# An attention pipeline's output stage: emitted in one piece, or one part per pipeline step

## The chip, the cores and the metric

The kernel runs on the 8 cores of one Trainium2 chip. Each core works on one of the 8 batch elements and exchanges nothing with the others. The metric is device time in microseconds of the slowest core for one execution.

## The reference

A backbone of four layers works on 4096 latent tokens and 256 context tokens per batch element, with 1024 channels. Layers 0 and 2 mix by a depthwise convolution beside a Fourier transform. Layers 1 and 3, which the change touches, do this:

```python
cb, cc, cx, cg, q, k, v, ag = _odd_proj(_pre(x, o_norm[i], sh, sc), o_w_in[i])
att = _window_attention(_apply_rope(q, cos, sin), _apply_rope(k, cos, sin), v, k_c, v_c, o_sink[i])
x = x + gt * _odd_out(cb, cc, cx, cg, att, ag, o_c_conv_w[i], o_w_out[i])

def _odd_out(cb, cc, cx, cg, att, ag, c_conv_w, w_out):
    y_c = cb * _dwconv(cc * cx, c_conv_w) * jax.nn.silu(cg)
    y_d = att * jax.nn.silu(ag)
    return jnp.concatenate([y_c, y_d], axis=-1) @ w_out
```

Attention has 8 query heads of 64 channels over 2 key heads. A query block of 128 tokens sees three key blocks of 128 around it, the 256 context keys, and a sink logit. In layer 1 the context tokens are updated too; in layer 3 they are not, and a final RMSNorm follows.

## The kernel before

An odd layer has two stages with a barrier between them. The first projects the inputs, block by block (8 blocks of 512 latent tokens, then one of 256 context tokens), and keeps keys and values in the on-chip memory. The second, in which everything here happens, is a software pipeline over units. A unit is one query block of 128 tokens and one head, so a full block of 512 tokens has 32 units; layer 1 has 272 units (the last 16 are the context's) and layer 3 has 256.

The loop at the end of `odd_layer` runs in steps. In step s it emits, in this order:

- `stA1(s)`: TensorE multiplies the mask, the keys and the context keys into two PSUM banks (the first matmul reads `mask_s` and stands at the start of a step in the trace); VectorE takes the row maximum (`TENSOR_REDUCE`, L1095); ScalarE takes the exponential (L153), from 642 columns.
- `stB(s-2)`: TensorE transposes the probabilities of unit s-2 in five pieces into bank 4 + (s % 2) (L143); they are copied out of that bank by ScalarE (`COPY`, L166), and for every third unit by VectorE (`COPY`, L168).
- `stC(s-4)`: TensorE multiplies the transposed probabilities with the values, five matmuls of 64 columns.
- whatever stands in `deferred` for that step.

Every engine works off its own instructions in order; a wait holds all that is queued behind it on that engine. The scheduler class adds the waits from the buffers that an operation reads and writes. A PSUM bank is one such buffer, so a matmul that opens a bank waits for the last reader of it. The semaphore of an engine counts its instructions in order.

After the eighth head of a query block, `fin2` is deferred by two steps: four transposes into bank 4 + (number of the query block % 2) and a VectorE multiplication into `mix`. For the last query block of a block, `fin2` also calls `stO3`, the output stage. It uses banks 4 and 5:

```python
for c in range(4):
    pc = bank(4 + c % 2)
...
out_stage(l, j, Wout, mx_, last, fin_bufs, banks=(4, 5))
```

These are four convolution pieces (3 matmuls of 512 columns and one VectorE multiplication each), eight output chunks (8 matmuls of 512 columns, then one `SCALAR_TENSOR_TENSOR` on VectorE, L162, that adds into `X`), then in layer 1 the store to `xres`, and in layer 3 the final norm: a square of 4096 columns on ScalarE, 32 matmuls of 2 columns, a square root on ScalarE, and for each of four token tiles eight transposes of 128 columns in single precision, two VectorE operations and a store. At last `load_block` fetches the inputs of the block after next over the GpSimd queue.

Of the kernel before, what the change touches and what calls it, by code (L numbers as in the profile page):

```python
# [10 lines left out]
AF = mybir.ActivationFunctionType  # L11
ALU = mybir.AluOpType
# [3 lines left out]
D = 1024  # L16
KC = 8
# [198 lines left out]
def build(L, LC, layers, dbg=False):  # L216
# [15 lines left out]
    s = Sched(nc)  # L232
# [8 lines left out]
    finbc_d = din("finbc", [128, D])  # L241
# [30 lines left out]
    out_d = nc.dram_tensor("out", [L, D], F32, kind="ExternalOutput").ap()  # L272
# [4 lines left out]
    xres = dscr("xres", [128, KC, T], F32)  # L277
# [10 lines left out]
    identf = sb("identf_s", [128, 128], F32)  # L288
    onesb = sb("onesb", [128, 128], BF16)
    ones512 = sb("ones512", [128, 128], BF16)  # L290
    epsc = sb("epsc", [128, 1], F32)
# [7 lines left out]
    modc = {l: sb("modc%d" % l, [128, 24, 2], F32) for l in layers}  # L299
# [15 lines left out]
    def bank(i):  # L315
        return PS[:, i * 512:(i + 1) * 512], bkb[i]

    ld = lambda out, in_, R, W: s.dma("sp", out, in_, R, W)
    st = lambda out, in_, R, W: s.dma("pool", out, in_, R, W)
# [162 lines left out]
                     e="act" if h == 0 else "dve")  # L482
        ld(xres.ap[:, :, t0:t0 + nt], xb.ap[:, :, :nt], [xb.b()], [xres.b(j)])

    def out_stage(l, j, Wout, mix, last, fin_bufs, banks=(4, 5, 6, 7), xb=None):
        stx, t0, nt = blocks[j]
        if xb is None:
            xb = X[j % 2]
        for m in range(KC):
            pb = bank(banks[m % len(banks)])  # L490
            p, b = pb
            for c in range(KC):
                s.mm(p[:, :nt], Wout.ap[:, c, m * 128:(m + 1) * 128], mix.ap[:, c, :nt], c == 0, c == KC - 1,
                     [Wout.b(), mix.b()], [b])
            s.stt(xb.ap[:, m, :nt], p[:, :nt], modc[l].ap[:, 16 + m, stx:stx + 1], xb.ap[:, m, :nt],
                  ALU.mult, ALU.add, [b, modc[l].b(), xb.b()], [xb.b()])
        if not last:
            st(xres.ap[:, :, t0:t0 + nt], xb.ap[:, :, :nt], [xb.b()], [xres.b(j)])
        elif stx == 0:
            finbc, sq, fst, TO = fin_bufs  # L500
            if not finbc.bufs:
                ld(finbc.ap, finbc_d, [], [finbc.b()])
            nti = nt // 128
            s.act(sq.ap[:, :, :nt], xb.ap[:, :, :nt], AF.Square, [xb.b()], [sq.b()])
            pss, pssb = bank(banks[-1])
            for i in range(nti):
                for c in range(KC):
                    s.mm(pss[:, 2 * i:2 * i + 2], sq.ap[:, c, i * 128:(i + 1) * 128], onesb.ap[:, 0:2],
                         c == 0, c == KC - 1, [sq.b(), onesb.b()], [pssb])
            s.act(fst.ap[:, 0:2 * nti], pss[:, 0:2 * nti], AF.Sqrt, [pssb, epsc.b()], [fst.b()],  # L510
                  bias=epsc.ap, scale=1.0 / D)
            s.op("dve", lambda e: e.reciprocal(fst.ap[:, 8:8 + 2 * nti], fst.ap[:, 0:2 * nti]), [fst.b()], [fst.b()])
            for i in range(nti):
                to = TO[i % 2]
                for h in range(2):
                    pt, ptb = bank(banks[-2 + h])
                    for c in range(4):
                        cc = h * 4 + c
                        s.tr(pt[:, c * 128:(c + 1) * 128], xb.ap[:, cc, i * 128:(i + 1) * 128], identf.ap,
                             [xb.b(), identf.b()], [ptb])  # L520
                    s.stt(to.ap[:, h * 512:(h + 1) * 512], pt, fst.ap[:, 8 + 2 * i:9 + 2 * i],
                          finbc.ap[:, h * 512:(h + 1) * 512], ALU.mult, ALU.mult,
                          [ptb, fst.b(), finbc.b()], [to.b()])
                st(out_d[t0 + i * 128:t0 + (i + 1) * 128, :], to.ap, [to.b()], [])

    def even_layer(l, last, nxt, first=False, win_pre=None):
        w = LW[l]
# [324 lines left out]
    def odd_layer(l, last, ctx_needed, nxt):  # L852
# [9 lines left out]
        sq = A.alloc([128, KC, 512], BF16)  # L862
# [33 lines left out]
        for j, (stx, t0, nt) in enumerate(blocks):  # L896
# [3 lines left out]
            h = hT[j % 2]  # L900
# [57 lines left out]
            for i in range(nt // 128):  # L958
                pt, ptb = bank(6 + i % 2)
# [11 lines left out]
        Wout = A.alloc([128, KC, D], BF16)  # L971
        diag = A.alloc([128, 4, 3, 128], BF16)
# [6 lines left out]
        mix = [A.alloc([128, 8, 512], BF16) for _ in range(2)]  # L979
# [3 lines left out]
        fin_bufs = None  # L983
        if last:
            fin_bufs = (A.alloc([128, D], F32), A.alloc([128, KC, 512], BF16), A.alloc([128, 16], F32),
                        [A.alloc([128, D], F32) for _ in range(2)])
# [17 lines left out]
        ablocks = [j for j, (stx, t0, nt) in enumerate(blocks) if stx == 0 or ctx_needed]  # L1004
# [9 lines left out]
        def load_block(j):  # L1014
            stx, t0, nt = blocks[j]
            sstart = 0 if stx == 0 else L
            send = L if stx == 0 else T
            xb = X[j % 2]
            st(xb.ap[:, :, :nt], xres.ap[:, :, t0:t0 + nt], [xres.b(j)], [xb.b()])
            gi = gDi[j % 2]  # L1020
            st(gi.ap[:, :, :nt], sB.ap[:, :, t0:t0 + nt], [sB.b(j)], [gi.b()])
            cbi = cbgi[j % 2]
            st(cbi.ap[:, :, :nt], sA.ap[:, :, t0:t0 + nt], [sA.b(j)], [cbi.b()])
            cxi = ccxi[j % 2]
            lo = max(t0 - 1, sstart)
            hi = min(t0 + nt + 1, send)
            nbr = [sC.b(jj) for jj in (j - 1, j, j + 1) if 0 <= jj < NB and blocks[jj][0] == stx]
            if lo == t0:
                s.op("dve", lambda e: e.memset(cxi.ap[:, :, 0:1], 0.0), [], [cxi.b()])
            if hi == t0 + nt:  # L1030
                s.op("dve", lambda e: e.memset(cxi.ap[:, :, nt + 1:nt + 2], 0.0), [], [cxi.b()])
            st(cxi.ap[:, :, lo - (t0 - 1):hi - (t0 - 1)], sC.ap[:, :, lo:hi], nbr, [cxi.b()])
# [31 lines left out]
        deferred = {}  # L1064
# [48 lines left out]
        def stC(u):  # L1113
            g = geom(u)
            j, qi, hh = g["j"], g["qi"], g["hh"]
            par, nk, hk = g["par"], g["nk"], g["hk"]
            o_ps, o_b = bank(6 + g["qbi"] % 2)
            vR = [Vf2.b(kb_) for kb_ in g["kbufs"]]
            nkt = nk // 128
            for t in range(nkt):  # L1120
                s.mm(o_ps[:, hh * 64:(hh + 1) * 64], pT_sb[u % 3].ap[:, t * 128:(t + 1) * 128],
                     Vf2.ap[:, g["ktiles"][t], hk * 64:(hk + 1) * 64], t == 0, t == nkt - 1,
                     [pT_sb[u % 3].b(0)] + vR, [o_b])
            if hh == 7:
                qbi = g["qbi"]
                sq_ = SQ[qbi % 2]
                asb = att_sb[qbi % 2]
                s.tt(asb.ap.rearrange("p (h d) -> p h d", h=8), o_ps.rearrange("p (h d) -> p h d", h=8),
                     sq_.ap[:, 5, :].unsqueeze(2).broadcast_to([128, 8, 64]), ALU.mult, [o_b, sq_.b(9)], [asb.b()])
                lastq = (qi == g["nt"] // 128 - 1)  # L1130

                def fin2(j=j, qi=qi, qbi=qbi, lastq=lastq):
                    asb_ = att_sb[qbi % 2]
                    mx_ = mix[j % 2]
                    gi = gDi[j % 2]
                    p7, p7b = bank(4 + qbi % 2)
                    p7v = p7.bitcast(BF16)
                    for c in range(4):
                        s.tr(p7v[:, c * 128:(c + 1) * 128], asb_.ap[:, c * 128:(c + 1) * 128], identb.ap,
                             [asb_.b(), identb.b()], [p7b])  # L1140
                    s.tt(mx_.ap[:, 4:8, qi * 128:(qi + 1) * 128], p7v[:, 0:512].rearrange("p (c q) -> p c q", c=4),
                         gi.ap[:, :, qi * 128:(qi + 1) * 128], ALU.mult, [p7b, gi.b()], [mx_.b()])
                    if lastq:
                        stO3(j)
                deferred.setdefault(u + 4 + 2, []).append(fin2)

        def stO3(j):
            stx, t0, nt = blocks[j]
            mx_ = mix[j % 2]
            cbi = cbgi[j % 2]  # L1150
            cxi = ccxi[j % 2]
            for c in range(4):
                pc = bank(4 + c % 2)
                for k in range(3):
                    s.mm(pc[0][:, :nt], diag.ap[:, c, k, :], cxi.ap[:, c, k:k + nt], k == 0, k == 2,
                         [diag.b(), cxi.b()], [pc[1]])
                s.tt(mx_.ap[:, c, :nt], pc[0][:, :nt], cbi.ap[:, c, :nt], ALU.mult, [pc[1], cbi.b()], [mx_.b()])
            out_stage(l, j, Wout, mx_, last, fin_bufs, banks=(4, 5))
            nx2 = ablocks.index(j) + 2
            if nx2 < len(ablocks):  # L1160
                load_block(ablocks[nx2])

        step = 0
        while step < NU + 4 or any(k >= step for k in deferred):
# [21 lines left out]
    for li, l in enumerate(layers):  # L1186
        last = (li == len(layers) - 1)
# [127 lines left out]
```

How the kernel before makes its waits and increments, by code:

```python
    def _wait(self, e, tok):  # L76
        k, sem, val, src = tok
        if src == "pe" and e == "pe":
            return
        if self.seen[e].get(k, 0) >= val:
            return
        self.eng[e].wait_ge(sem, val)
        self.seen[e][k] = val
# [19 lines left out]
    def op(self, e, fn, R=(), W=()):  # L103
        self._deps(e, R, W)
        inst = fn(self.eng[e])
        self.cnt[e] += 1
        inst.then_inc(self.sem[e], 1)
        self._commit((self.semk[e], self.sem[e], self.cnt[e], e), R, W)
# [1 line left out]
    def dma(self, q, out, in_, R=(), W=(), **kw):  # L110
        self._deps(q, R, W)
        i = self.rpos[q]
        self.rpos[q] = (i + 1) % self.NRING
        sem = self.ring[q][i]
        k = self.ringk[q][i]
        prev = self.rval[q][i]
        if prev:
            self._wait(q, (k, sem, prev, "dma"))
        inst = self.eng[q].dma_start(out=out, in_=in_, **kw)
        inst.then_inc(sem, 16)
        self.rval[q][i] = prev + 16
        self._commit((k, sem, prev + 16, "dma"), R, W)
```

## Time and profile before

| quantity | value |
| --- | --- |
| runs | 4970.52 and 5032.25 us, median 5001.38 us |
| profiled execution | 4973.7 us, span of its slowest core 4972.4 us |
| spans of the 8 cores | 4937.0 to 4972.4 us |
| TensorE busy | 3913.2 us (79%) |
| VectorE busy | 1979.7 us (40%) |
| ScalarE busy | 1661.6 us (33%) |
| mean granted TensorE clock, per core | 0.905 to 0.912 |

The profile is that of core 1. The attention pipeline of layer 1 lies between 1911 and 2530 us of its span, that of layer 3 between 4270 us and the end. A granted clock of 1.00 is the upper level of TensorE (2.4 GHz), 0.50 the lower (1.2 GHz).

### The profile page before, as it was taken

Reading aid. Unit: us, or ns where it says so; the run is one execution under the profiler, and the core shown is the slowest. Engines: PE = TensorE matmul, PEld = TensorE weight load, DVE = VectorE, ACT = ScalarE, POOL = GpSimd, SP = SyncE. Lnnn points to the kernel's source line nnn. Section 1 sums busy time; section 2 is a strip of 40 time slices with the busy share of each in tenths; the row PEclk is TensorE's granted clock in tenths of the full one; section 3 lists DMA queues with packets and bytes.
Section 4 is the critical chain, followed back from the end, with each engine's and each line's share of the span. In section 5 each row is a group of like instructions: output and inputs, shape, how many; then the busy total and the mean of one; then the engine's idle time right before and its main releaser. Section 6 shows DMA issues by size and latency. Waiting matters only on the chain.

```text
span 4972.4 us, 75994 instructions; the slowest of 8 cores (4937.0 to 4972.4 us)
## 1 busy us (share of the span) xinstructions
PE 3913.2 (79%) x26536; PEld 2224.8 (45%) x26536; DVE 1979.7 (40%) x3068; ACT 1661.6 (33%) x2642; POOL 465.0 (9%) x511
## 2 busy tenths in 40 slices
PE   2989599789569996777769959969874999577776
PEld 1444344665324444544434434456542444344454
DVE  1333344122235444656533333311222444455564
ACT  1545233000023334655535523310002333455463
POOL 1000000000101221000010000000001112100000
PEclk9999799899879998999879979979987999899888
DMA  8333212854552224332433221166436321321210
GB/s 154 123 127 106 51 44 49 253 182 170 152 130 89 89 68 109 120 112 78 112 109 104 77 56 43 49 205 221 161 140 138 106 89 64 96 101 54 94 61 37
DMA packets 223621, 537.60 MB, mean 108 GB/s; under 512 B 51024, under 2 KB 69840, under 8 KB 215056
## 3 DMA queue, kind: packets, MB, share of 16 engines
q0 software_dynamic: 103568, 323.02, 22.4%
q1 hardware_dynamic: 119680, 209.72, 13.1%
q8 instruction: 221, 3.62, 0.3%
q14 instruction: 152, 1.25, 0.1%
HBM read 424.94 MB, written 167.25 MB: 119 GB/s over the span
## 4 chain that ended last, share of the span: by engine, by line
PE 68%; DVE 8%; DMA 8%; issue 6%; ACT 5%; POOL 3%; another core or an unknown queue 1%; DVEq 0%; SPq 0%; POOLq 0%; ACTq 0%
PE ps L140 63%; PE ps L143 5%; ACT arena L153 4%; POOL arena L156 3%; DVE arena L156 3%; DMA arena<-sD 2%; DVE arena L159 1%; DMA X<-xres 1%; DVE arena L887 1%; DMA arena<-wmod 1%; DVE arena L162 1%; ACT arena L166 1%; DMA arena<-x 1%; DMA arena<-pqd 1%
## 5 line engine op out<-in xcount | busy, mean ns | idle before, releaser
L140 PE MATMUL ps<-arena 128*128 128x512 bf16 (+4 forms) x19564 | 3406.7, 328 | 372.6 <-DVE arena L156 111.6
L140 PEld LDWEIGHTS ps<-arena 128*128 128x128 bf16 x19564 | 1793.7, 100 | 1814.1 <-issue 556.1
L153 ACT ACTIVATE arena<-ps,biasW 128x512 f32<-128x512 f32 (+3 forms) x614 | 410.4, 671 | 725.3 <-PE ps L140 682.3
L153 ACT ACTIVATE arena<-ps,arena 128x642 bf16<-128x642 f32 (+2 forms) x528 | 414.4, 785 | 343.5 <-PE ps L140 186.9
L1095 DVE TENSOR_REDUCE arena<-ps 128x1 f32<-128x642 f32 (+2 forms) x528 | 424.5, 805 | 227.9 <-PE ps L143 111.4
L166 ACT COPY arena<-ps 128x640 bf16<-128x640 bf16 (+3 forms) x369 | 252.4, 684 | 766.0 <-PE ps L140 706.4
L156 DVE TENSOR_TENSOR arena<-ps,arena 128x512 bf16<-128x512 f32 (+4 forms) x328 | 215.9, 666 | 538.1 <-PE ps L140 231.0
L143 PE MATMUL ps<-identb_s,arena 128*128 128x128 bf16 x2892 | 282.4, 228 | 158.6 <-ACT arena L166 71.7
L162 DVE SCALAR_TENSOR_TENSOR X<-ps,modc,X 128x512 f32<-128x512 f32 (+1 forms) x280 | 203.8, 728 | 330.0 <-PE ps L140 327.7
L153 ACT ACT_TABLE_LOAD x156 | 200.1, 1283 | 354.7 <-PE ps L140 135.3
L162 DVE SCALAR_TENSOR_TENSOR arena<-ps,biasW,arena 128x512 bf16<-128x512 f32 (+1 forms) x208 | 149.1, 717 | 340.8 <-PE ps L140 275.3
L143 PEld LDWEIGHTS ps<-identb_s,arena 128*128 128x128 bf16 x2892 | 184.0, 101 | 219.7 <-issue 182.4
L140 PE MATMUL ps<-mask_s,identb_s 128*128 128x384 bf16 (+1 forms) x512 | 174.2, 340 | 128.0 <-ACT arena L153 111.5
L153 ACT ACTIVATE arena<-X 128x4096 bf16<-128x4096 f32 (+1 forms) x44 | 152.1, 3458 | 348.5 <-DMA X<-xres 173.6
L153 ACT ACTIVATE arena<-ps,v_s 128x512 f32<-128x512 f32 (+3 forms) x144 | 87.9, 662 | 444.0 <-PE ps L140 444.0
L162 DVE SCALAR_TENSOR_TENSOR arena<-X,G,ps 128x512 bf16<-128x512 f32 (+1 forms) x288 | 205.4, 713 | 19.4 <-DVE arena L162 1.4
L168 DVE CAST arena<-ps 128x512 bf16<-128x512 f32 (+2 forms) x74 | 46.8, 660 | 375.5 <-ACT arena L166 189.0
L156 DVE TENSOR_TENSOR arena<-arena 128x512 f32<-128x512 f32 x192 | 131.3, 684 | 119.7 <-POOL arena L156 119.7
L140 PE MATMUL ps<-arena,onesb 128*128 128x512 bf16 (+1 forms) x288 | 71.3, 394 | 107.5 <-ACT arena L153 107.5
L156 POOL TENSOR_TENSOR arena<-arena 128x512 f32<-128x512 f32 x96 | 140.6, 1464 | 130.0 <-DVE arena L887 128.3
L168 DVE CAST arena<-arena 128x512 bf16<-128x512 f32 (+1 forms) x76 | 31.0, 408 | 304.4 <-ACT arena L153 304.4
L426 DVE RECIPROCAL ps<-arena 128x512 f32<-128x512 f32 (+1 forms) x32 | 101.1, 3161 | 107.6 <-ACT arena L153 107.6
(78 smaller groups left out, 1778.5 us busy)
## 6 DMA issues: line engine op xcount, KB each, us to landing
arena<-dfth SPq DMA_DIRECT2D x64, 1024.0 KB, 10.1
X<-xres POOLq DMA_DIRECT2D x32, 2048.0 KB, 19.6
xres<-X POOLq DMA_DIRECT2D x24, 2048.0 KB, 8.6
X<-xres SPq DMA_DIRECT2D x24, 2048.0 KB, 10.6
arena<-win POOLq DMA_DIRECT2D x10, 2048.0 KB, 36.9
pqd<-arena POOLq DMA_DIRECT2D x68, 256.0 KB, 2.6
arena<-x SPq DMA_DIRECT2D x32, 512.0 KB, 8.6
xres<-X SPq DMA_DIRECT2D x8, 2048.0 KB, 8.5
```

Of the source, the lines that this page charges most:

```text
L140: self.op("pe", lambda e: e.matmul(out, lhsT, rhs, start=start, stop=stop), R, W)
L143: self.op("pe", lambda e: e.transpose(out, in_, ident), R, W)
L153: self.op("act", lambda e: e.activation(out, in_, func, **kw), R, W)
L156: self.op(e, lambda g: g.tensor_tensor(out, in0, in1, op), R, W)
L159: self.op(e, lambda g: g.tensor_scalar(out, in0, s1, s2, op0, op1), R, W)
L162: self.op("dve", lambda g: g.scalar_tensor_tensor(out, in0, scalar, in1, op0, op1), R, W)
L166: self.op("act", lambda g: g.copy(out, in_), R, W)
L168: self.op(e, lambda g: g.tensor_copy(out, in_), R, W)
L426: s.op("dve", lambda e: e.reciprocal(p1[:, :nt], rt.ap[:, :nt]), [rt.b()], [p1b])
L887: s.op("dve", lambda e: e.stream_shuffle(sh.ap[:, :nt], src.ap[:, :nt], SHM), [src.b()], [sh.b()])
L1095: s.op("dve", lambda e: e.reduce_max(sq_.ap[:, 1, hh:hh + 1], Sr, AX.X, negate=True), Sb, [sq_.b(hh)])
```

## The change

`out_stage` becomes a list of functions, `out_stage_parts`: one for each of the eight chunks, then one for the store, or for the statistics and one for each of the four token tiles. `stO3` builds the list of its four convolution pieces, those parts, and a last one that calls `load_block`. It emits none of them at once: part k goes into `deferred` for step step0 + 1 + k, where step0 is the step in which `fin2` runs. The even layers still emit all parts one after the other through `out_stage`. No instruction is added or dropped.

```diff
-    def out_stage(l, j, Wout, mix, last, fin_bufs, banks=(4, 5, 6, 7), xb=None):
+    def out_stage_parts(l, j, Wout, mix, last, fin_bufs, banks=(4, 5, 6, 7), xb=None):
...
+        parts = []
+
+        def mk_chunk(m):
+            def f():
+                p, b = bank(banks[m % len(banks)])
+                for c in range(KC):
+                    s.mm(p[:, :nt], Wout.ap[:, c, m * 128:(m + 1) * 128], mix.ap[:, c, :nt], c == 0, c == KC - 1,
+                         [Wout.b(), mix.b()], [b])
+                s.stt(xb.ap[:, m, :nt], p[:, :nt], modc[l].ap[:, 16 + m, stx:stx + 1], xb.ap[:, m, :nt],
+                      ALU.mult, ALU.add, [b, modc[l].b(), xb.b()], [xb.b()])
+            return f
         for m in range(KC):
...
+            parts.append(mk_chunk(m))
         if not last:
-            st(xres.ap[:, :, t0:t0 + nt], xb.ap[:, :, :nt], [xb.b()], [xres.b(j)])
+            parts.append(lambda: st(xres.ap[:, :, t0:t0 + nt], xb.ap[:, :, :nt], [xb.b()], [xres.b(j)]))
...
-                        stO3(j)
+                        stO3(j, u + 4 + 2)
...
             for c in range(4):
-                pc = bank(4 + c % 2)
...
+                parts.append(mk_conv(c))
+            parts += out_stage_parts(l, j, Wout, mx_, last, fin_bufs, banks=(4, 5))
+
+            def f_next():
+                nx2 = ablocks.index(j) + 2
+                if nx2 < len(ablocks):
+                    load_block(ablocks[nx2])
+            parts.append(f_next)
+            for k_, fn in enumerate(parts):
+                deferred.setdefault(step0 + 1 + k_, []).append(fn)
```

## Rows read from the trace of the kernel before

**Rows 1.** Windows, the attention pipelines of layers 1 and 3

```profile
core 1: us, PE busy (x) PEld busy (x) DVE busy (x) ACT busy (x) POOL busy (x), PEclk, DMA share, GB/s
1911.00:2530.00 619.00, 474.54 (x4658) 305.31 (x4656) 361.94 (x580) 325.14 (x727) 33.97 (x42) 0.92 0.36 105
4270.00:4980.00 710.00, 514.39 (x4783) 332.55 (x4781) 394.38 (x604) 360.40 (x710) 36.31 (x56) 0.89 0.19 68
```

**Rows 2.** Timeline, VectorE, undisturbed steps of layer 1 (first and eighth maximum)

```profile
start us, us, engine line op out<-in xcount [idle before <-releaser]
2080.19 0.83 DVE L1095 TENSOR_REDUCE arena<-ps 128x1 f32<-128x642 f32 x1
...
2089.80 0.83 DVE L1095 TENSOR_REDUCE arena<-ps 128x1 f32<-128x642 f32 x1 [0.55 <-PE ps L140]
```

**Rows 3.** Timeline, a step whose fin2 shares the step's bank, copy on ScalarE

```profile
2014.61 0.32 PE L140 MATMUL ps<-mask_s,identb_s 128*128 128x384 bf16 x1 [0.21 <-ACT arena L153]
...
2015.35 0.83 DVE L1095 TENSOR_REDUCE arena<-ps 128x1 f32<-128x642 f32 x1
...
2017.11 0.68 ACT L166 COPY arena<-ps 128x640 bf16<-128x640 bf16 x1
...
2017.94 0.38 PE L143 MATMUL ps<-identb_s,arena 128*128 128x128 bf16 x4 [2.16 <-ACT arena L166]
...
2018.16 0.33 PE L140 MATMUL ps<-mask_s,identb_s 128*128 128x384 bf16 x1
```

**Rows 4.** Timeline, the same in a step whose copy is VectorE's

```profile
1971.94 0.32 PE L140 MATMUL ps<-mask_s,identb_s 128*128 128x384 bf16 x1 [0.33 <-ACT arena L153]
...
1973.42 0.48 DVE L168 COPY arena<-ps 128x640 bf16<-128x640 bf16 x1
...
1974.05 0.38 PE L143 MATMUL ps<-identb_s,arena 128*128 128x128 bf16 x4 [0.94 <-DVE arena L168]
```

**Rows 5.** Timeline, the output stage of block 0 and the step after

```profile
1974.28 1.64 PE L140 MATMUL ps<-arena 128*128 128x512 bf16 x6
...
1978.79 13.97 PE L140 MATMUL ps<-arena 128*128 128x512 bf16 x64 [1.01 <-DVE arena L156]
...
1992.60 0.33 PE L140 MATMUL ps<-mask_s,identb_s 128*128 128x384 bf16 x1
...
1992.94 0.75 DVE L162 SCALAR_TENSOR_TENSOR X<-ps,modc,X 128x512 f32<-128x512 f32 x1 [0.98 <-PE ps L140]
...
1993.61 1.55 DVE L1095 TENSOR_REDUCE arena<-ps 128x1 f32<-128x642 f32 x2
...
1995.36 0.69 ACT L166 COPY arena<-ps 128x640 bf16<-128x640 bf16 x1
```

**Rows 6.** Windows, granted clock after the wait of Rows 3, and in convolution pieces

```profile
2019.30:2022.60 3.30, 3.09 (x29) 2.42 (x28) 2.19 (x4) 2.26 (x5) 0.00 (x0) 0.50 0.11 27
...
2050.60:2053.00 2.40, 2.40 (x7) 0.72 (x6) 1.38 (x2) 0.00 (x0) 0.00 (x0) 0.50 1.11 209
```

**Rows 7.** Timeline, VectorE, two convolution pieces inside that second window

```profile
2051.00 0.69 DVE L156 TENSOR_TENSOR arena<-ps,arena 128x512 bf16<-128x512 f32 x1 [0.52 <-PE ps L140]
2052.28 0.69 DVE L156 TENSOR_TENSOR arena<-ps,arena 128x512 bf16<-128x512 f32 x1 [0.59 <-PE ps L140]
```

**Rows 8.** Timeline, layer 3, the statistics, the tiles and the step after them

```profile
4603.81 3.62 ACT L153 ACTIVATE arena<-X 128x4096 bf16<-128x4096 f32 x1 [19.23 <-DVE X L162]
...
4608.99 1.28 ACT L153 ACT_TABLE_LOAD   x1 [1.56 <-PE ps L143]
...
4618.56 1.94 PE L143 MATMUL ps<-identf_s,X 128*128 128x128 f32 x8 [2.46 <-DVE arena L162]
...
4620.30 0.53 PE L140 MATMUL ps<-mask_s,identb_s 128*128 128x384 bf16 x1
...
4621.50 0.83 DVE L1095 TENSOR_REDUCE arena<-ps 128x1 f32<-128x642 f32 x1
...
4622.46 1.28 ACT L153 ACT_TABLE_LOAD   x1 [11.90 <-DVE arena L1095]
```

**Rows 9.** Timeline, ScalarE, an exponential of the context's units in layer 1

```profile
2500.96 0.48 ACT L153 ACTIVATE arena<-ps,arena 128x258 bf16<-128x258 f32 x1 [0.40 <-DVE arena L1095]
```

**Rows 10.** The page's DMA issues

```profile
X<-xres POOLq DMA_DIRECT2D x32, 2048.0 KB, 19.6
```

More of the change, by code:

```diff
@@ L488, in out_stage @@
             xb = X[j % 2]
-        for m in range(KC):
[L490 to L496, printed above, removed]
+        parts = []
@@ L497, in out_stage @@
+        for m in range(KC):
+            parts.append(mk_chunk(m))
         if not last:
-            st(xres.ap[:, :, t0:t0 + nt], xb.ap[:, :, :nt], [xb.b()], [xres.b(j)])
+            parts.append(lambda: st(xres.ap[:, :, t0:t0 + nt], xb.ap[:, :, :nt], [xb.b()], [xres.b(j)]))
         elif stx == 0:
             finbc, sq, fst, TO = fin_bufs
-            if not finbc.bufs:
-                ld(finbc.ap, finbc_d, [], [finbc.b()])
             nti = nt // 128
-            s.act(sq.ap[:, :, :nt], xb.ap[:, :, :nt], AF.Square, [xb.b()], [sq.b()])
@@ L505, in out_stage @@
-            pss, pssb = bank(banks[-1])
-            for i in range(nti):
[L507 to L524, printed above, removed]
+            def f_stats():
+                if not finbc.bufs:
+                    ld(finbc.ap, finbc_d, [], [finbc.b()])
+                s.act(sq.ap[:, :, :nt], xb.ap[:, :, :nt], AF.Square, [xb.b()], [sq.b()])
+                pss, pssb = bank(banks[-1])
+                for i in range(nti):
+                    for c in range(KC):
+                        s.mm(pss[:, 2 * i:2 * i + 2], sq.ap[:, c, i * 128:(i + 1) * 128], onesb.ap[:, 0:2],
+                             c == 0, c == KC - 1, [sq.b(), onesb.b()], [pssb])
+                s.act(fst.ap[:, 0:2 * nti], pss[:, 0:2 * nti], AF.Sqrt, [pssb, epsc.b()], [fst.b()],
+                      bias=epsc.ap, scale=1.0 / D)
+                s.op("dve", lambda e: e.reciprocal(fst.ap[:, 8:8 + 2 * nti], fst.ap[:, 0:2 * nti]),
+                     [fst.b()], [fst.b()])
@@ new lines, in out_stage_parts, with mk_tile, f @@
+            parts.append(f_stats)
+            def mk_tile(i):
+                def f():
+                    to = TO[i % 2]
+                    for h in range(2):
+                        pt, ptb = bank(banks[-2 + h])
+                        for c in range(4):
+                            cc = h * 4 + c
+                            s.tr(pt[:, c * 128:(c + 1) * 128], xb.ap[:, cc, i * 128:(i + 1) * 128], identf.ap,
+                                 [xb.b(), identf.b()], [ptb])
+                        s.stt(to.ap[:, h * 512:(h + 1) * 512], pt, fst.ap[:, 8 + 2 * i:9 + 2 * i],
+                              finbc.ap[:, h * 512:(h + 1) * 512], ALU.mult, ALU.mult,
+                              [ptb, fst.b(), finbc.b()], [to.b()])
+                    st(out_d[t0 + i * 128:t0 + (i + 1) * 128, :], to.ap, [to.b()], [])
+                return f
@@ L526, in even_layer, with out_stage @@
+            for i in range(nti):
+                parts.append(mk_tile(i))
+        return parts
+    def out_stage(l, j, Wout, mix, last, fin_bufs, banks=(4, 5, 6, 7), xb=None):
+        for fn in out_stage_parts(l, j, Wout, mix, last, fin_bufs, banks=banks, xb=xb):
+            fn()
     def even_layer(l, last, nxt, first=False, win_pre=None):
@@ L1143, in fin2, with stO3 @@
                     if lastq:
-                        stO3(j)
+                        stO3(j, u + 4 + 2)
                 deferred.setdefault(u + 4 + 2, []).append(fin2)
-        def stO3(j):
+        def stO3(j, step0):
             stx, t0, nt = blocks[j]
@@ L1151, in stO3, with mk_conv, f @@
             cxi = ccxi[j % 2]
-            for c in range(4):
-                pc = bank(4 + c % 2)
[L1154 to L1161, printed above, removed]
+            parts = []
+            def mk_conv(c):
+                def f():
+                    pc = bank(4 + c % 2)
+                    for k in range(3):
+                        s.mm(pc[0][:, :nt], diag.ap[:, c, k, :], cxi.ap[:, c, k:k + nt], k == 0, k == 2,
+                             [diag.b(), cxi.b()], [pc[1]])
+                    s.tt(mx_.ap[:, c, :nt], pc[0][:, :nt], cbi.ap[:, c, :nt], ALU.mult, [pc[1], cbi.b()], [mx_.b()])
+                return f
+            for c in range(4):
+                parts.append(mk_conv(c))
[7 more added lines that the diff above has]
+                deferred.setdefault(step0 + 1 + k_, []).append(fn)
         step = 0
```

## The prediction

> **What bounds the kernel now.** I read the windows first, to see how much of the span the change can reach: the two attention pipelines take 619 and 710 us, and TensorE is busy in 77% and 72% of them, VectorE in 58% and 56%, ScalarE in 53% and 51% [rows 1]. No engine is full, so the timeline had to say what ends a step. In undisturbed steps the maxima of VectorE follow each other at (2089.80 - 2080.19) / 7 = 1.37 us [rows 2]. A step holds 1.17 us of TensorE work (from 2014.61 to the start of an idle time, 2.16 us before 2017.94 [rows 3]), so TensorE has 0.2 us to spare in each; the rest is the chain from the maximum over the exponential to the copy. The output stage stands in this as a block: TensorE starts it at 1974.28 and begins the next step at 1992.60, 18.3 us later, 13.8 us of which are the 64 chunk matmuls, 1.73 us per chunk [rows 5]. ScalarE has nothing to do meanwhile; in layer 3 it is idle for 19.23 us before the square [rows 8].
>
> The most telling view is the timeline of two steps that the kernel has already, those where `fin2` opens a bank. In step s the transposes of `stB(s-2)` go to bank 4 + s % 2, and their copy is emitted behind the maximum and the exponential of unit s. Where `fin2` takes the same bank it must wait for that copy. In one such step TensorE begins at 2014.61, the maximum at 2015.35, the copy on ScalarE at 2017.11, and the transposes of `fin2` at 2017.94, after 2.16 us of idle time: 3.33 us from the step's start [rows 3]. Where the copy is VectorE's, the wait ends 2.11 us after the start, with 0.94 us idle [rows 4]. This is what any matmul pays that opens the step's own bank at the end of the step.
>
> **The change part by part.** Which bank does a moved part open? The last unit of a block is odd, `fin2` runs six steps after it, and part 0 in the step after that, an even one. Convolution piece c takes bank 4 + c % 2 and comes in a step of parity c % 2; chunk m takes bank 4 + m % 2 in a step of parity m % 2. So each of the 12 parts opens exactly the bank that the same step's transposes have just filled. Before, this wait came once per block; now it comes 12 times, and TensorE can't start the next step's `stA1` meanwhile, because that stands behind the waiting matmul. VectorE and ScalarE run dry behind it.
>
> The price of a step with a part. The start is a little later than in rows 3, since VectorE first drains the part before: after the last chunk of block 0 TensorE begins at 1992.60, VectorE's chunk operation runs from 1992.94, the maximum starts at 1993.61, and the ScalarE copy at 1995.36, 2.76 us after the start [rows 5]. With the 0.83 us from the copy's start to TensorE's [rows 3] the wait ends at 3.59 us. With a VectorE copy it is 1.01 us to the maximum, and from there 1.37 us as in rows 4 (2.11 less 0.74), 2.38 us. One copy in three is VectorE's: (2 x 3.59 + 2.38) / 3 = 3.19 us. On top come the part's own matmuls, 1.73 us for a chunk, 0.65 us for a convolution piece (three at 0.216 us). Twelve steps then take 12 x 3.19 + 8 x 1.73 + 4 x 0.65 = 54.7 us. Before, the same twelve steps took 12 x 1.37 = 16.4 us and the block of work 18.3 us, 34.7 us. That adds 20.0 us per block at full clock.
>
> How many blocks: in layer 1 blocks 0 to 6 lie over full units. Block 7 lies over the context's units, whose exponential has 258 columns for 642 and takes 0.48 us [rows 9]; I take 15 us, between 0 and 20. The context block has no units behind it, its parts run one after the other as before. In layer 3 blocks 0 to 6 overlap and block 7 doesn't. That is 7 x 20.0 + 15 + 7 x 20.0 = 295 us.
>
> The five further steps of layer 3 (statistics and four tiles). Before, from the square's start at 4603.81 to the next step at 4620.30 are 16.5 us, some 1.1 us for the last chunk's operation precede (0.34 us to its start and 0.75 us for it [rows 5]) and a table load of 1.28 us for the exponential follows [rows 8]: 18.9 us, and with five steps of 1.37 us 25.7 us. After: the statistics step waits 3.2 us, then 3.6 us for the square and 1.6 us for its matmuls and the hand-over (from the square's end at 4607.43 to the table load at 4608.99 [rows 8]); the first tile's step holds two table loads, the exponential and the copy (some 4.1 us) and four transposes, 1.0 us; three more have 3.2 us and 1.9, 1.0 and 1.9 us of transposes (eight take 1.94 us [rows 8]). Together 8.4 + 5.1 + 14.4 = 27.9 us, about 2 us more; but the stores of the tiles, which hold up VectorE in the block of work, are spread too. I take no net change; the bounds are -3 and +3 us per block, 21 us in all.
>
> The clock. A wait of this size has a second cost that the trace shows: after the 2.16 us of idle time the granted clock is 0.50, the lower level, in the stretch that follows [rows 3, 6].  At the lower level a convolution piece takes 2052.28 - 2051.00 = 1.28 us [rows 7], twice 0.65, so a chunk takes 3.46 us; and the maximum starts 1.20 us after the step [rows 8], 0.19 us later. A low chunk step costs 1.92 us more, a low convolution step 0.82 us, all twelve 18.6 us. In that stretch TensorE is busy for 3.09 of 3.30 us [rows 6], and since the mean over the layer is 0.92 [rows 1] the level must return soon after such work; chunks of 3.46 us are work of this kind, so it should swing. I take four steps in ten as low, 7.4 us per block, 15 x 7.4 = 111 us; none and all are the bounds (0 and 279 us). The Trainium skill, "TensorE: Matmul & The Clock Gate", section "A second HAM failure mode: psum-queue depth-cycling", says that small idle times between matmul groups that cycle through PSUM banks make the clock swing between its two states; the row of 0.50 after the wait agrees.
>
> Moved transfers: `load_block` leaves 14 steps later in layer 1 and 18 in layer 3. Its largest transfer lands 19.6 us after the issue [rows 10], and the first reader, the new block's first `fin2`, comes over 20 steps (28 us at 1.37 us) later, so I cost it at nothing; without this cover it would be some 10 us per block. The store's wait holds only GpSimd's queue, where nothing else is urgent.
>
> The sum, against the profiled execution: 4974 + 295 + 0 + 111 = 5380 us. The median of the runs shown is 27 us above that execution with only two runs; I stay with the execution and say 5375 us.
>
> **The rivals.** (a) The waits as priced, but the clock stays at its upper level: 4974 + 295 = about 5270 us. For it: the two idle times of a step are separated by 1.73 us or more of full work; against it: one single wait was enough [rows 6].
>
> (b) The waits, with the clock low nearly throughout: 4974 + 295 + 279 = about 5550 us. Against it: long chunks bring it back.
>
> (c) On the other side: the copies are done when a part reaches its bank. The place is the first matmul of each part, the price 0, and it decides from the point where the copy ends within 1.2 us of the step's start rather than 3.6. Steps are then TensorE's: 12 x 1.17 + 8 x 1.73 + 4 x 0.65 = 30.5 us instead of 34.7, 4.2 us less per block, 63 us over 15, and with the square and the tiles under other work in layer 3 up to 5 us per block more: about 4900 us, not slower. For it speaks ScalarE's idle time of 19 us per block [rows 8]; against it rows 3 and 4, where the same wait is seen. The Trainium skill's "Perfetto Trace Analysis", section "Optimization Strategy", says that interleaving stretches with different most-contended engines may improve performance; by that rule this rival would come true. TensorE's 0.2 us to spare per step leaves it little here.
>
> (d) The parts don't overlap with anything, because they fall behind the units: 4974 us, no change. Step numbers speak against it, 37 + 32j in the middle of the loop.
>
> **How the numbers follow.** 0.58 for the forecast, 0.20 for (a), 0.10 for (b), 0.10 for (c), 0.02 for (d). A measurement of this kernel can tell about 2% from no change, 100 us. (c) lies within that or just beyond it: 0.04 faster, 0.08 the same with (d), 0.88 slower. The range leaves out (c), (d) and most of (b), and takes (a) in with a margin for the tails of layer 3: 5220 to 5490 us.
>
> **What would show it.** In the changed trace: steps with 8 matmuls of 512 columns whose first waits 2.4 us for the ScalarE copy or 1.2 us for VectorE's; step starts 5.3 or 4.1 us apart at full clock; a mean granted clock in both pipelines below 0.92 and 0.89; TensorE's busy share falling while its full-clock work is unchanged; both pipelines longer, layer 1 by some 210 us, layer 3 by some 190. The prediction is wrong if the chunks start right behind `stC`, if a copy gets ahead of the exponential, or if the even layers move at all.

## The result and the profile after

The changed kernel is slower: 1.075 times the time of the kernel before (95% interval 1.067 to 1.083), where the forecast of 5375 us over the 4974 us of the profiled execution is 1.081. In some executions of either kernel, the profiled one of the changed kernel among them, a die runs at a lower granted clock, so ratios are of the other executions (5356 to 5400 us for the changed kernel) and what follows is read on core 5, of the die that kept its clock. Its span went from 4956.9 to 5348.7 us, by 391.8 us.

The windows of the two attention pipelines of the changed kernel answer to [rows 1]:

```profile
core 5: us, PE busy (x) PEld busy (x) DVE busy (x) ACT busy (x) POOL busy (x), PEclk, DMA share, GB/s
1908.00:2718.00 810.00, 532.31 (x4659) 326.63 (x4659) 357.53 (x580) 328.85 (x727) 33.97 (x42) 0.83 0.27 80
4457.00:5349.00 892.00, 562.48 (x4736) 360.97 (x4736) 386.82 (x598) 361.28 (x699) 36.32 (x56) 0.80 0.14 51
```

VectorE and ScalarE have the same work as before in both, while both stretches are longer: each is a chain of waits, and TensorE's busy share has fallen from 77% and 72% to 66% and 63%. Its busy time has risen, and the clock column says why: 0.83 and 0.80 for 0.92 and 0.89 (core 5 of the kernel before shows the same 0.92 and 0.89 as core 1). The start of each stage is marked by a memset on GpSimd. By these marks layer 1's pipeline took 636.7 us before (1884.61 to 2521.31) and takes 831.7 us (1888.54 to 2720.25), 195 us more; from the mark of layer 3's pipeline to the last instruction it was 725.4 us and is 922.4 us, 197 us more. Together that is 392 us, the whole difference of the spans: nothing is left for the even layers. The marks, first in the kernel before, then in the changed one:

```profile
1884.61 1.88 POOL L1001 MEMSET arena<- 128x1024 bf16 x2
...
2521.31 14.82 POOL L553 MEMSET arena<- 128x17664 bf16 x1 [5.70 <-DMA xres<-X]
...
4231.48 1.86 POOL L1001 MEMSET arena<- 128x1024 bf16 x2
```

```profile
1888.54 1.88 POOL L1020 MEMSET arena<- 128x1024 bf16 x2
...
2720.25 14.82 POOL L572 MEMSET arena<- 128x17664 bf16 x1 [6.37 <-DMA xres<-X]
...
4426.32 1.86 POOL L1020 MEMSET arena<- 128x1024 bf16 x2
```

The timeline of the changed kernel, two chunk steps of block 1 in layer 1, answers to [rows 3, 4]. A step begins with the matmul that reads `mask_s`:

```profile
2099.76 0.33 PE L140 MATMUL ps<-mask_s,identb_s 128*128 128x384 bf16 x1
...
2101.49 0.48 DVE L168 COPY arena<-ps 128x640 bf16<-128x640 bf16 x1
...
2102.12 1.89 PE L140 MATMUL ps<-arena 128*128 128x512 bf16 x8 [1.32 <-DVE arena L168]
...
2103.85 0.33 PE L140 MATMUL ps<-mask_s,identb_s 128*128 128x384 bf16 x1
2104.19 0.75 DVE L162 SCALAR_TENSOR_TENSOR X<-ps,modc,X 128x512 f32<-128x512 f32 x1 [2.21 <-PE ps L140]
...
2107.43 1.89 PE L140 MATMUL ps<-arena 128*128 128x512 bf16 x8 [2.54 <-ACT arena L166]
```

The eight matmuls of a chunk start 2.36 us after their step where the copy is VectorE's and 3.58 us where it is ScalarE's (2107.43 - 2103.85); the idle time in brackets names the copy of the same step as what ended it. Fourteen microseconds earlier the same shape stands at the lower clock, where the mask's matmul takes 0.52 us for 0.33 and the chunk 3.57 us:

```profile
2085.61 0.52 PE L140 MATMUL ps<-mask_s,identb_s 128*128 128x384 bf16 x1
...
2089.40 3.57 PE L140 MATMUL ps<-arena 128*128 128x512 bf16 x8 [1.90 <-ACT arena L166]
```

The groups by form add this up over layer 1. The same 608 matmuls, first in the kernel before, then in the changed one (busy time and mean; idle time ahead of them and what ended it):

```profile
L140 PE MATMUL ps<-arena 128*128 128x512 bf16 x608 | 143.3, 393 | 10.3 <-DVE arena L156 10.2
```

```profile
L140 PE MATMUL ps<-arena 128*128 128x512 bf16 x608 | 207.2, 495 | 169.9 <-ACT arena L166 139.3 <-DVE arena L168 23.7 <-DVE arena L1130 6.9
```

Two changes stand in these rows side by side: 160 us more of idle time, nearly all of it ended by the copies L166 and L168, and 64 us more of busy time for the same work, which is the lower clock.

### The profile page after: what moved, and what is told of

It is laid out like the page before. It is cut to its first block, busy times and chain, and to the rows that moved or that the text cites. A ratio compares the mean times of both kernels' runs of the same rounds, so it can differ in the third digit from the quotient of the medians.

```text
span 5609.0 us, 75551 instructions; the slowest of 8 cores (5327.9 to 5609.0 us)
## 1 busy us (share of the span) xinstructions
PE 4304.9 (77%) x26536; PEld 2363.4 (42%) x26536; DVE 1971.7 (35%) x3068; ACT 1673.4 (30%) x2642; POOL 465.2 (8%) x511
## 3 DMA queue, kind: packets, MB, share of 16 engines
q8 instruction: 219, 3.59, 0.3%
## 4 chain that ended last, share of the span: by engine, by line
PE 69%; DVE 9%; issue 7%; DMA 6%; ACT 6%; POOL 2%; another core or an unknown queue 1%; DVEq 0%; ACTq 0%; SPq 0%; POOLq 0%
PE ps L140 65%; PE ps L143 5%; ACT arena L153 3%; DVE arena L1114 2%; ACT arena L166 2%; DVE arena L156 2%; POOL arena L156 2%; DMA arena<-sD 1%; DVE arena L159 1%; DVE arena L162 1%; DMA X<-xres 1%; DMA arena<-wmod 1%; DVE arena L168 1%; DMA arena<-x 1%; DVE arena L906 1%
## 5 line engine op out<-in xcount | busy, mean ns | idle before, releaser
L140 PE MATMUL ps<-arena 128*128 128x512 bf16 (+4 forms) x19564 | 3803.3, 352 | 663.9 <-ACT arena L166 270.9
L140 PEld LDWEIGHTS ps<-arena 128*128 128x128 bf16 x19564 | 1894.6, 105 | 2334.7 <-issue 1591.6
L166 ACT COPY arena<-ps 128x640 bf16<-128x640 bf16 (+3 forms) x369 | 252.1, 683 | 827.7 <-PE ps L140 827.7
L156 DVE TENSOR_TENSOR arena<-ps,arena 128x512 bf16<-128x512 f32 (+4 forms) x328 | 215.9, 666 | 690.7 <-PE ps L140 369.8
L143 PE MATMUL ps<-identb_s,arena 128*128 128x128 bf16 x2892 | 296.0, 236 | 151.4 <-ACT arena L166 49.7
L143 PEld LDWEIGHTS ps<-identb_s,arena 128*128 128x128 bf16 x2892 | 195.9, 105 | 213.4 <-issue 186.9
L140 PE MATMUL ps<-mask_s,identb_s 128*128 128x384 bf16 (+1 forms) x512 | 189.3, 370 | 78.4 <-ACT arena L153 62.6
L168 DVE CAST arena<-ps 128x512 bf16<-128x512 f32 (+2 forms) x74 | 46.6, 660 | 408.4 <-PE ps L140 271.2
L156 DVE TENSOR_TENSOR arena<-arena 128x512 f32<-128x512 f32 x192 | 131.3, 684 | 119.3 <-POOL arena L156 119.3
L156 POOL TENSOR_TENSOR arena<-arena 128x512 f32<-128x512 f32 x96 | 140.8, 1466 | 146.1 <-DVE arena L906 145.2
L168 DVE CAST arena<-arena 128x512 bf16<-128x512 f32 (+1 forms) x76 | 30.8, 406 | 347.0 <-ACT arena L153 347.0
## 6 DMA issues: line engine op xcount, KB each, us to landing
X<-xres POOLq DMA_DIRECT2D x32, 2048.0 KB, 16.1
```

The costliest lines, as they stand in the source:

```text
L140: self.op("pe", lambda e: e.matmul(out, lhsT, rhs, start=start, stop=stop), R, W)
L143: self.op("pe", lambda e: e.transpose(out, in_, ident), R, W)
L156: self.op(e, lambda g: g.tensor_tensor(out, in0, in1, op), R, W)
L166: self.op("act", lambda g: g.copy(out, in_), R, W)
L168: self.op(e, lambda g: g.tensor_copy(out, in_), R, W)
```

## The experiments

Every ratio below is to the kernel before, measured beside it, with its 95% interval. Ratios within some 1% of 1 are read as different from 1 only where the interval leaves 1 out, and they are small. The explanation under test: a part waits for the copy out of the PSUM bank that its own step has filled, and that copy is queued behind the maximum and the exponential; the clock falls in these idle times and adds to it.

**One step later.** The least edit that flips the parity.

```diff
-                deferred.setdefault(step0 + 1 + k_, []).append(fn)
+                deferred.setdefault(step0 + 2 + k_, []).append(fn)
```

> The changed kernel with every part one step later, so that part k falls in a step of the other parity and opens the bank that the same step's transposes do not use. Nothing else differs. Theory (own-bank wait): the waits of 2.4 and 1.2 us behind the copy go; what stays is that the next step's transposes wait about 0.5 us for VectorE to drain the part. Twelve steps then take about 36.5 us against 34.7 us before: 0.985 to 1.02 of the kernel before, about 1.005. Rival (the price is TensorE's and VectorE's added work per step, whatever the bank): stays at 1.06 to 1.08.

Measured: 1.0064 (1.0036 to 1.0092). The 608 matmuls now have 7.3 us of idle time ahead of them in layer 1, not 169.9:

```profile
L140 PE MATMUL ps<-arena 128*128 128x512 bf16 x608 | 155.2, 395 | 7.3 <-ACT arena L166 7.2
```

And the timeline shows the wait that stays, the next step's transposes behind VectorE's drain of the part, 0.63 us where 0.5 was expected:

```profile
2067.28 0.75 DVE L162 SCALAR_TENSOR_TENSOR X<-ps,modc,X 128x512 f32<-128x512 f32 x1 [1.45 <-PE ps L140]
...
2068.18 0.44 PE L143 MATMUL ps<-identb_s,arena 128*128 128x128 bf16 x5 [0.63 <-DVE X L162]
```

The same matmuls, one step later, cost 0.6% where they cost 7.5%. TensorE's added work per step is not the price.

**The other bank, the same step.**

```diff
-                    pc = bank(4 + c % 2)
+                    pc = bank(5 - c % 2)
...
-            parts += out_stage_parts(l, j, Wout, mx_, last, fin_bufs, banks=(4, 5))
+            parts += out_stage_parts(l, j, Wout, mx_, last, fin_bufs, banks=(5, 4))
```

> The changed kernel with parts in the same steps, but banks 4 and 5 exchanged for all parts. The theory of the own-bank wait expects the same as for the run with parts one step later, within 1% of it (about 1.005 of the kernel before). If the step in which a part falls mattered and not the bank, this run would stay at 1.06 to 1.08 while the other fell.

Measured: 1.0053 (1.0031 to 1.0076), the same as one step later within the intervals. Here the parts stay in the steps of the changed kernel and only the bank differs: it is the bank and not the step.

**The copy first.** The bank is shared as in the changed kernel, but nothing of its own step stands ahead of the copy.

```diff
-            if step < NU:
-                stA1(step)
             if 0 <= step - 2 < NU:
                 stB(step - 2)
+            if step < NU:
+                stA1(step)
```

> The changed kernel with the transposes and the copy of unit s-2 emitted ahead of the scores, maximum and exponential of unit s. Parts open the same bank as in the changed kernel, but the copy is no longer queued behind the maximum and the exponential on its engine. Theory (the wait is long because of what stands ahead of the copy): waits shrink to near 0, part steps take 1.2 us plus the part, 0.97 to 1.02 of the kernel before, about 0.99. If the sharing of a bank cost by itself: 1.05 or more.

Measured: 0.9983 (0.9964 to 1.0002). The chunk waits 0.38 us for the same copy, not 2.5 us:

```profile
2071.39 0.44 PE L143 MATMUL ps<-identb_s,arena 128*128 128x128 bf16 x5
...
2071.97 0.69 ACT L166 COPY arena<-ps 128x640 bf16<-128x640 bf16 x1 [0.69 <-PE ps L143]
...
2072.81 1.89 PE L140 MATMUL ps<-arena 128*128 128x512 bf16 x8 [0.38 <-ACT arena L166]
```

So sharing the bank is harmless where its reader is not queued behind the maximum and the exponential.

**The wait filled with matmuls.** This asks for the clock's share. The kernel does extra matmuls whose results nobody uses.

```diff
+            def filler(st_):
+                def f():
+                    if st_ - 2 < NU and st_ < NU:
+                        ob = bank(4 + (st_ + 1) % 2)
+                        for _ in range(5 if (st_ - 2) % 3 == 2 else 10):
+                            s.mm(ob[0], identb.ap, Wout.ap[:, 0, 0:512], True, True, [identb.b(), Wout.b()], [ob[1]])
+                return f
             for k_, fn in enumerate(parts):
+                if k_ < 12:
+                    deferred.setdefault(step0 + 1 + k_, []).append(filler(step0 + 1 + k_))
                 deferred.setdefault(step0 + 1 + k_, []).append(fn)
```

> The changed kernel, with idle time of TensorE filled: ahead of each of the 12 matmul parts stand 10 matmuls of 512 columns (2.16 us at full clock) into the other bank, or 5 where the copy is VectorE's; nobody reads them. The wait itself stays. Theory (waits plus about 111 us of lower clock): the granted clock in both pipelines rises to 0.95 or more and the time falls to about 1.055 of the kernel before (1.04 to 1.065). Rival (the clock makes most of the loss): 1.03 or less. Rival (the clock costs nothing of note): 1.075 or more.

Measured: 1.0608 (1.0576 to 1.0639). TensorE does more work, and the kernel is faster than the changed one, whose ratio was 1.075. The windows of the two pipelines:

```profile
1908.00:2685.00 777.00, 631.05 (x5439) 371.73 (x5439) 355.43 (x586) 329.04 (x727) 38.12 (x48) 0.95 0.31 87
4430.00:5268.00 838.00, 651.26 (x5399) 394.75 (x5396) 381.90 (x593) 357.21 (x691) 36.31 (x56) 0.89 0.15 53
```

The clock came back to 0.95 in layer 1, as expected, and to 0.89 in layer 3, where 0.95 was expected too; the statistics and the tiles have idle times there that were not filled. The kernel before has 0.92 and 0.89, so neither pipeline is below it any more. The waits are all there: in the filled run two chunk steps take 5.31 and 4.09 us, the 5.3 and 4.1 us that the prediction gave for full clock:

```profile
2102.15 0.33 PE L140 MATMUL ps<-mask_s,identb_s 128*128 128x384 bf16 x1
...
2107.46 0.33 PE L140 MATMUL ps<-mask_s,identb_s 128*128 128x384 bf16 x1
...
2111.55 0.33 PE L140 MATMUL ps<-mask_s,identb_s 128*128 128x384 bf16 x1
```

Both rivals fall: the clock does cost, and it is the smaller share. What the waits cost with the clock held up is 0.0608 x 4979 = 303 us (4979 us is the kernel before, beside this run). What filling gave back is 0.0142 x 4979 = 71 us by the ratios, with an uncertainty of some 40 us, most of it from the interval of the 1.075. The traces have it closer: on core 5 the two pipelines of the filled run are 50 and 48 us shorter than those of the changed kernel.

**Part of the parts.** First only the convolution pieces are spread, then only the chunks and what follows.

```diff
+            rest = parts[4:]
+            parts = parts[:4] + [lambda: [fn() for fn in rest]]
             for k_, fn in enumerate(parts):
```

> Only the four convolution pieces are spread, one per step; the eight chunks and all behind them come in one block in the step after. Theory (each matmul part that opens its step's own bank costs a step of 3.2 us plus its matmuls): 4 x (3.19 + 0.65 - 1.37) = 9.9 us per block, less the 4.5 us that the pieces take in the block of work, plus some 2.4 us since the first chunk waits too, and 1 to 2 us of clock: about 9 us in 15 blocks, 1.02 to 1.03 of the kernel before. Rival (only the long chunks cost, since they make a step TensorE's): 1.00 to 1.01.

Measured: 1.0263 (1.0168 to 1.0359), as expected; the interval is wide, as the ratio rests on two executions.

```diff
+            for fn in parts[:4]:
+                fn()
+            parts = parts[4:]
             for k_, fn in enumerate(parts):
```

> The four convolution pieces are emitted at once behind fin2, as before the change; the eight chunks and what follows are spread. Theory: 8 x (3.19 + 1.73 - 1.37) - 13.8 = 14.6 us per block and 4 to 6 us of clock: 1.05 to 1.06 of the kernel before, so that the excess over 1 of this run and of the one with the convolution pieces alone add up to about that of the whole change (0.075). Rival (the loss is made once per block, by the first waits): about as slow as the whole change.

Measured: 1.0546 (1.0454 to 1.0637), again from two executions. Together 0.081, against 0.075 for the whole change; the intervals are wide enough to hold equality. The matmuls' idle time in layer 1 goes the same way, first the run with the convolution pieces, then that with the chunks:

```profile
L140 PE MATMUL ps<-arena 128*128 128x512 bf16 x608 | 162.3, 426 | 66.9 <-ACT arena L166 56.0 <-DVE arena L168 8.8 <-DVE arena L1130 2.1
```

```profile
L140 PE MATMUL ps<-arena 128*128 128x512 bf16 x608 | 198.9, 484 | 131.7 <-ACT arena L166 105.3 <-DVE arena L168 22.8 <-DVE arena L1130 2.5
```

The price is paid per part that opens a bank. Pieces of 0.65 us cost their share, which rules out that only the long chunks make a step too long.

**The wait that the kernel before has.** `fin2` always in bank 4, the output stage in one block.

```diff
-                    p7, p7b = bank(4 + qbi % 2)
+                    p7, p7b = bank(4)
```

> The kernel before, with fin2 always in bank 4, which its step's transposes never use, since fin2 runs in odd steps. It takes out the waits that the prediction's price was read from: 33 of the 66 fin2 open their own step's bank (about 1.75 us each on average), the others already wait about 0.8 us. Theory: 33 x 0.95 = 31 us and some lower clock less: 0.985 to 0.995 of the kernel before. If own-bank waits did not count on the path: 1.00.

Measured: 0.9922 (0.9875 to 0.9969), 39 us, with 31 us and a little clock expected. The waits from which the prediction took its price [rows 3, 4] were on the path there too.

**Parts after the scores.** In the other bank, and emitted between `stA1(s)` and `stB(s-2)`.

```diff
             if step < NU:
                 stA1(step)
+            for fn in early.pop(step, []):
+                fn()
             if 0 <= step - 2 < NU:
                 stB(step - 2)
```

> The changed kernel with each part emitted between the scores of unit s and the transposes of unit s-2, and with banks 4 and 5 exchanged. The bank's last copy then lies a step back, and the next step's transposes come 1.3 us of TensorE's work after the part, longer than the 1.1 us in which VectorE drains it. Theory: no wait is left in a part's step, it takes 2.9 to 3.1 us for a chunk, and 0 to 5 us per block are won: 0.985 to 1.00 of the kernel before. Rival (VectorE's or ScalarE's order makes a new wait of the same size): 1.01 or more.

Measured: 0.9935 (0.9891 to 0.9978). This is the spreading without its waits, and now it gains, though only 0.65%. The timeline of two steps shows what is left, 0.40 us for the copy that the step before left in that bank:

```profile
2065.54 0.69 ACT L166 COPY arena<-ps 128x640 bf16<-128x640 bf16 x1 [0.62 <-PE ps L140]
...
2066.37 1.89 PE L140 MATMUL ps<-arena 128*128 128x512 bf16 x8 [0.40 <-ACT arena L166]
...
2069.52 1.89 PE L140 MATMUL ps<-arena 128*128 128x512 bf16 x8 [0.40 <-ACT arena L166]
```

Step follows step after 3.15 us (2069.52 - 2066.37), slightly over the 2.9 to 3.1 expected.

**Both together.** The run before with `fin2` in bank 4.

> Parts after the scores and in the other bank (0.9935), with fin2 always in bank 4 as in the run of the kernel before (0.9922). Theory: the two touch different waits, so they add: 0.98 to 0.99, the fastest. If both lived from the same wait: 0.993.

Measured: 0.9895 (0.9820 to 0.9969), the lowest ratio of all runs and below both kernels, its slowest core at 4931.4 us in the profiled execution. The interval holds the sum of the two (0.986) and either one, so that they add is not shown.

**The copy first, without the change.** The control for the 0.9983.

> The kernel before, with the transposes and the copy of unit s-2 emitted ahead of the scores of unit s; the output stage in one block as before. It is the control for the changed kernel with the same exchange (0.998): if the exchange only removes the waits of the spread parts and fin2, this run is 0.985 to 1.00 and the spreading itself is worth nothing under it; if the exchange slows the undisturbed steps and the spreading wins that back, this run is above 1.005.

Measured: 1.0072 (1.0023 to 1.0120), the second case of the expectation. Undisturbed steps are longer there. In one stretch, two maxima of that run, six steps apart, are 9.16 us apart, 1.53 us a step, for 1.37 us in [rows 2]:

```profile
2084.20 0.83 DVE L1095 TENSOR_REDUCE arena<-ps 128x1 f32<-128x642 f32 x1 [0.66 <-PE ps L140]
...
2093.36 0.83 DVE L1095 TENSOR_REDUCE arena<-ps 128x1 f32<-128x642 f32 x1
```

With the copy first, spreading took the time from 1.0072 to 0.9983, about 0.9% (the two were measured on different chips, but each against the kernel before, and the intervals don't meet); the exchange itself eats that up.

**The copy first and `fin2` in bank 4.**

> The changed kernel with the copy first (0.998), and fin2 always in bank 4. With the copy first the own bank is drained early and fin2 no longer waits long for it in either bank, so the theory expects little: 0.99 to 1.00.

Measured: 1.0019 (0.9964 to 1.0074), not better than 0.9983. The groups by form in layer 1 show the transposes waiting 34.9 us for `fin2`'s multiplication (L156); with the copy first and alternating banks it was 20.3 us. First the alternating banks, then bank 4:

```profile
L143 PE MATMUL ps<-identb_s,arena 128*128 128x128 bf16 x1432 | 131.3, 222 | 108.6 <-ACT arena L153 69.7 <-DVE arena L156 20.3 <-ACT arena L166 12.3
```

```profile
L143 PE MATMUL ps<-identb_s,arena 128*128 128x128 bf16 x1426 | 132.6, 223 | 110.8 <-ACT arena L153 71.5 <-DVE arena L156 34.9 <-DVE arena L1114 2.4
```

With the transposes at the head of the next, even, step, bank 4 is just the bank that they need: the choice that gained 39 us in one order of emission gains nothing in the other. That it loses is not shown: the intervals of the two runs overlap, the transposes' idle time is nearly the same in all (110.8 and 108.6 us), and by the marks on core 5 layer 1's pipeline took 633.9 us with bank 4 and 636.9 us with alternating banks.

## Why the prediction was right

**The bank and the parity.** Shown. Each of the 12 parts waited for its own step's copy, and moving either the bank or the step by one took the loss from 7.5% to 0.5 or 0.6%.

**The price of a wait.** 3.59 and 2.38 us were forecast, 3.58 and 2.36 us are in the trace, 3.79 us at the lower clock for 3.78. The step that had the most weight was read off waits that the kernel before already had, in `fin2`, and off the step behind its output stage.

**The twelve steps.** 62.1 us were forecast for them, 54.7 us at full clock and 7.4 us for the clock. On core 5 of the changed kernel they take 59.7 to 66.9 us in the fourteen blocks that lie over full units, 62.7 us on average, and in the filled run 55.8 us on average, so filling gave back 6.9 us per block. Block 1 of layer 1, from the first part's step to the step after the last chunk, first in the changed kernel (64.34 us), then in the filled run (56.05 us):

```profile
2069.66 0.52 PE L140 MATMUL ps<-mask_s,identb_s 128*128 128x384 bf16 x1
...
2134.00 0.33 PE L140 MATMUL ps<-mask_s,identb_s 128*128 128x384 bf16 x1
```

```profile
2081.38 0.52 PE L140 MATMUL ps<-mask_s,identb_s 128*128 128x384 bf16 x1
...
2137.43 0.33 PE L140 MATMUL ps<-mask_s,identb_s 128*128 128x384 bf16 x1
```

**The same work before, 34.7 us.** This term was too small. The forecast took twelve undisturbed steps of 1.37 us. On core 5 of the kernel before, the twelve steps behind the output stage take 16.7 to 21.9 us in layer 1, since `fin2` with its own waits falls into them, and with the block of work it is 37.7 us on average over seven blocks. In layer 1, where the twelve steps are 63.9 us long on average, a block adds 26.2 us, for 27.4 us in the forecast: two errors, of 3.0 and 1.8 us, that partly cancel.

**295 us of waits.** With the clock held up the loss was 303 us. So close a match is luck in part: the parts cost less than forecast, and the statistics and tiles, put at nothing, cost some 38 us, as follows.

**The clock, 111 us.** The direction was right, and the size is near. In a stretch of parts in layer 1 the granted clock is 0.79, which with two levels is 42% of the time at the lower one, for the four steps in ten of the forecast. The 512-column matmuls of layer 1 are 64 us longer, near the 59 us (8 x 7.4) of that term. Filling the waits gave back 71 +- 40 us by the ratios and 98 us by the marks of the two pipelines, while the statistics and tiles, which were not filled, kept their idle times.

**The statistics and tiles of layer 3, no net change.** Here a term was mis-sized. The timeline of the changed kernel in block 0, from the statistics step to the step after the last tile:

```profile
4564.96 0.33 PE L140 MATMUL ps<-mask_s,identb_s 128*128 128x384 bf16 x1
...
4573.02 0.48 PE L140 MATMUL ps<-mask_s,identb_s 128*128 128x384 bf16 x1
...
4575.14 0.20 DVE L519 RECIPROCAL arena<-arena 128x8 f32<-128x8 f32 x1 [8.36 <-ACT arena L153]
...
4575.31 0.83 DVE L1114 TENSOR_REDUCE arena<-ps 128x1 f32<-128x642 f32 x1
...
4576.26 1.28 ACT L153 ACT_TABLE_LOAD   x1 [1.23 <-DVE arena L1114]
...
4579.17 1.08 PE L143 MATMUL ps<-identf_s,X 128*128 128x128 f32 x4 [2.13 <-ACT arena L166]
4580.05 0.53 PE L140 MATMUL ps<-mask_s,identb_s 128*128 128x384 bf16 x1
...
4596.22 0.53 PE L140 MATMUL ps<-mask_s,identb_s 128*128 128x384 bf16 x1
```

The five steps take 31.3 us here (4596.22 - 4564.96). This block is one of the longest: the seven take 27.5 to 31.3 us on core 5, 29.8 us on average, for 27.9 us in the forecast. The 25.7 us for before were also read from the longest block: from the last chunk's matmuls to the next step it has 17.5 us, and the seven blocks have 16.3 us on average on its core 1 and 16.1 us on core 5, which makes 24.3 us of the 25.7. So it is some 5.5 us more per block, 38 us in seven, outside the forecast's bounds of 3 us. In the block shown, the statistics step is as forecast (8.1 us for 8.4). The first tile's step takes 7.0 us for 5.1: the reciprocal holds VectorE until the square root is done, and the next unit's maximum is queued behind it, so the exponential comes late, a wait that the forecast had not named; it is about as long (7.0 to 7.4 us) in five of the seven blocks, and 4.7 us in the other two. The other three take 16.2 us for 14.4, with the mask's matmul at 0.53 us, the lower clock, at each of their starts; the forecast had priced them at full clock. The other bank or step does not cure this part: in the run one step later the five steps still take 29.0 us on average, and of the 37 us by which the two pipelines of its core 5 are longer than before, 25 us are layer 3's.

**The layers.** 195 us for 214 forecast in layer 1, 197 us for 192 in layer 3, where the 38 us above are included. The twelve parts together thus cost less than forecast. In layer 1 seven blocks of 26.2 us make 184 us, which leaves 11 us for block 7 over the context's units, for 22 us in the forecast.

**Moved transfers.** Costed at nothing, and rightly: the run one step later has them later still and costs 0.6% in all, so they hold no large part of the loss.

**The rivals.** That the clock stays up (5270 us) is about what the filled run made by force. The rival on the other side needed a copy that ends before its part arrives. That is not the case in the changed kernel; where it was made so, by emission after the scores in the other bank, the time was 0.9935 of before, 32 us less for the 74 us of that rival. The Trainium skill's rule on interleaving ("Perfetto Trace Analysis", "Optimization Strategy") holds in this sense: the gain exists, is small here, as TensorE has little to spare in a step, and was buried under waits that cost ten times as much (303 us for 32 us). That the little room in a step is what keeps it small is argued, not shown.

## What to carry to other kernels

Before work is moved into the steps of a software pipeline, list for each moved part which buffer it opens, who read that buffer last, and what is queued ahead of that reader on its engine. A wait that a kernel pays once per block in one place is paid once per part after the spreading, and a parity that happens to match makes it the worst in every step. Look for the price in the trace of before: a smaller operation that already opens the same buffer at the same place shows it. Here it gave the wait to 0.02 us, once the later start of a step behind a part was added.

## What the runs showed of the hardware

Adding matmuls that nobody reads made a kernel faster: 10 or 5 matmuls of 512 columns ahead of each of the parts brought the granted clock in layer 1 from 0.83 to 0.95 and the whole from 1.075 to 1.061, though the waits themselves were left in place. In the changed kernel TensorE stood idle for 1.0 to 2.5 us ahead of each part in the window below, and its granted clock there was 0.79; behind the last part, from 2137 to 2166 us, it was 1.00:

```profile
2074.00:2134.00 60.00, 37.72 (x230) 19.30 (x229) 18.56 (x29) 14.42 (x30) 0.00 (x0) 0.79 0.12 23
```
